# Moving four pieces of a two-block kernel: k's first tiles into the second transpositions, wider turns of k, the first attention gate ahead of q's last turn, scores inside the fourth attention gate

## What is computed

```python
h = concatenate([meta, x])                          # 16 + 1024 = 1040 positions
u = rmsnorm(h, norm_g)
f_in, f_gate, q, k, v, a_gate = split(u @ w_in)     # 512, 512, 512, 128, 128, 512
f_out = fourier_branch(f_in, w_fmix, b_fmix) * silu(f_gate)
q = apply_rope(rmsnorm(q, q_g), cos, sin)           # 8 heads of 64
k = apply_rope(rmsnorm(k, k_g), cos, sin)           # 2 heads of 64
s = q @ k.T * 64 ** -0.5
a_out = (softmax(s) @ v) * silu(a_gate)
h = h + concatenate([f_out, a_out]) @ w_out
h = rmsnorm(h, final_g)
# second block: stick-breaking attention, gated convolution, FFN
```

## Time and profile before

| | |
|---|---|
| median of 3 runs | 2277.32 us (2276.4 to 2278.12) |
| the profiled execution | 2277.11 us, its span 2275.1 us |
| PE busy | 2138.6 us (94%) |
| DVE / ACT / POOL busy | 50% / 37% / 30% |
| chain that ended last | PE 84%, DVE 10%, ACT 3%, issue 2%, DMA 1% |

### The profile page before, as it was taken

The page is one execution under the profiler, slowest core; times in us unless marked ns, Lnnn a source line. Parts: engine busy times, 40 slices in busy tenths (PEclk is TensorE's granted clock), DMA queues, the critical chain, the costliest instruction groups (busy, mean ns, idle before and its releaser), DMA issues.

```text
span 2275.1 us, 27632 instructions
## 1 busy us (share of the span) xinstructions
PE 2138.6 (94%) x10609; PEld 1769.5 (78%) x10609; DVE 1136.8 (50%) x1547; ACT 831.4 (37%) x1477; POOL 673.5 (30%) x527
## 2 busy tenths in 40 slices
PE   6898998999998999898998999989999999999996
...
DMA packets 142919, 164.65 MB, mean 72 GB/s; under 512 B 7091, under 2 KB 108999, under 8 KB 142823
## 3 DMA queue, kind: packets, MB, share of 16 engines
...
...
## 4 chain that ended last, share of the span: by engine, by line
PE 84%; DVE 10%; ACT 3%; issue 2%; DMA 1%; ACTq 0%; DVEq 0%
PE psum L589 18%; PE psum L591 18%; PE psum L590 17%; PE psum L886 15%; PE psum L798 3%; PE psum L809 3%; PE psum L824 1%; PE psum L825 1%; PE psum L826 1%; PE psum L923 1%; PE psum L907 1%; DVE softplus_part L1994 1%; PE psum L599 1%; PE psum L940 1%; PE psum L908 1%
## 5 line engine op out<-in xcount | busy, mean ns | idle before, releaser
L534 POOL TENSOR_TENSOR w_ring<-w_staging,zero 128x8 fp32r<-128x8 f32 x172 | 47.3, 275 | 1548.6 <-PE psum L591 1055.3
L537 POOL TENSOR_TENSOR w_ring<-w_staging,w_ring 128x1024 fp32r<-128x1024 f32 (+1 forms) x172 | 440.3, 2560 | 14.4
L886 PE MATMUL psum<-h,w_ring 128*128 128x512 f32 x1728 | 440.8, 406 | 0.7 <-ACT v L1380 0.7
L886 PEld LDWEIGHTS psum<-h,w_ring 128*128 128x128 f32 x1728 | 322.3, 193 | 69.3 <-ACT v L1380 1.1
L589 PE MATMUL psum<-ffn_in,w_ring 128*128 128x512 f32 x672 | 265.4, 395 | 0.0
L591 PE MATMUL psum<-ffn_in,w_ring 128*128 128x512 f32 x672 | 264.2, 393 | 0.0
L590 PE MATMUL psum<-ffn_in,w_ring 128*128 128x512 f32 x672 | 263.8, 393 | 0.0
L2116 DVE SCALAR_TENSOR_TENSOR up_buf<-psum,vectors,up_buf 128x1023 f32<-128x1023 f32 x44 | 56.4, 1283 | 308.3 <-ACT up_buf L1598 308.3
L535 POOL TENSOR_SCALAR w_ring<-w_staging 128x1016 fp32r<-128x1016 f32 (+1 forms) x172 | 183.0, 1064 | 0.0
L591 PEld LDWEIGHTS psum<-ffn_in,w_ring 128*128 128x128 f32 x672 | 126.0, 188 | 30.5
L590 PEld LDWEIGHTS psum<-ffn_in,w_ring 128*128 128x128 f32 x672 | 126.3, 188 | 29.3
...
## 6 DMA issues: line engine op xcount, KB each, us to landing
...
```

The source lines that it names most:

```text
L537: pool.tensor_tensor(lo[:, 0:width], WS[:, s, 0:width], plain(hi[:, 0:width]), ALU.subtract).then_inc(S["w_split"], 1)
L886: ins = pe.matmul(mix_bank(h), (sl if x == 2 else sh)[:, P * k:P * k + P], ml if x == 1 else mh, start=m == 0, stop=m == UNIT // 2 - 1)
```

## The change

- POOL makes the three MEMSETs of v_hi_ones_lo instead of DVE, as soon as the last tile of u is transposed, and two more chunks are split ahead of its loop, so that they stand before them.
- DVE normalises tiles 0 and 1 of the second transpositions amid the last four pairs of the DFT's results (`again`), each behind two pairs.
- Tiles 0 and 1 of k are squared, summed, guessed and rotated amid tiles 4 to 8 of the second transpositions (`k_square`, `k_guess` on ACT, `rotate`, `k_rotate` on DVE: the same instructions as before, named). Tiles 2 to 8 stay in the later loop.
- PE turns k's tiles 0 and 1 straight behind the last `kv_unit`; the other seven turns stand one behind every 15 products of the Fourier gates.
- `a_gate(0)` stands ahead of the last tile of q on ACT (`q_hi(TT - 1)`, line 1244 before) and on DVE (`q_lo(TT - 1)`, line 1866 before).
- PE's fourth attention gate is made in two halves, with `scores(1)` and `turn_probs(0)` between them. ACT makes `probs_hi(0)` in step 2, then the sigmoid of gate 3; DVE makes its MEMSET in step 1 and the product of gate 3 in step 3; the gate's store and the first loads of the gates move from steps 2 and 4 to 4 and 5.

```diff
-            peeled = C_KV + 2
+            peeled = C_KV + 4
...
+            pool.wait_ge(S["nt_mm"], N_A1 + KTILES)
+            pool.memset(plain(VV[:, TT, :, :]), 0.0).then_inc(S["vv_set"], 1)
+            pool.memset(plain(VV[:, 0:TT, :, DH:2 * DH]), 1.0).then_inc(S["vv_set"], 1)
+            pool.wait_ge(S["vv_set"], 2)
+            pool.memset(plain(VV[0:META, TT, :, DH:2 * DH]), 1.0).then_inc(S["vv_set"], 1)
...
-            def fm_unit(c, mov, banks, between=None):
+            def fm_unit(c, mov, banks, between=None, halves=range(2)):
...
-                for h in range(2):
+                for h in halves:
...
+            turn_k(0)
+            turn_k(1)
+
+            def turn_beside(f, m):
+
+                i = 2 * KT * f + m
+                if i % 5 == 4 and i // 5 + 2 < KTILES:
+                    turn_k(i // 5 + 2)
 
             for f in range(4):
                 if f == 1:
                     settle(tm=T_Q)
                 elif f == 3:
                     settle(fm=U_FGATE + 1)
-                fm_unit(C_FGATE + f, a1_half, F_GATE_PAIRS[f],
-                        lambda m: turn_k(4 * f + m // 4) if m % 4 == 3 and 4 * f + m // 4 < KTILES else None)
+                fm_unit(C_FGATE + f, a1_half, F_GATE_PAIRS[f], lambda m: turn_beside(f, m))
...
             pe.wait_ge(S["pr_done"], TT)
             scores(0)
             settle(fm=U_AGATE + 2)
-            fm_unit(C_AGATE + 3, a1_half, A_GATE_PAIRS[3])
+            fm_unit(C_AGATE + 3, a1_half, A_GATE_PAIRS[3], halves=range(1))
+            scores(1)
             settle(fm=U_AGATE + 3)
-            for i in range(1, HEADS * TT + 3):
+            turn_probs(0)
+            fm_unit(C_AGATE + 3, a1_half, A_GATE_PAIRS[3], halves=range(1, 2))
+            for i in range(2, HEADS * TT + 3):
...
+            def k_square(u):
+                rows = tokens_of(u)[1]
+                act.wait_ge(S["tm_free"], T_KV + u + 1)
+                act.activation(KSQ[0:rows, u % 2, 0:P], KV[0:rows, u, 0:P], ACT.Square).then_inc(S["pr_sq"], 1)
+
+            def k_guess(u):
+                guess(tokens_of(u)[1], 8 * (u % 2), KV_HEADS, 1.0 / DH, True)
...
+                if t in (4, 6):
+                    k_square(t // 2 - 2)
+                elif t in (5, 7):
+                    k_guess(t // 2 - 2)
...
+                    if u >= 2:
+                        k_square(u)
                     act.activation(VV[0:rows, u, :, 0:DH], KV[0:rows, u, P:2 * P].rearrange("p (g d) -> p g d", g=KV_HEADS),
                                    ACT.Copy).then_inc(S["kv_vhi"], 1)
-                    guess(rows, col, KV_HEADS, 1.0 / DH, True)
+                    if u >= 2:
+                        k_guess(u)
...
             a_gate(0)
+            q_hi(TT - 1)
             a_gate(1)
...
-                if i == 1:
+                if i == 2:
+                    act.wait_ge(S["pt_zero"], 1)
+                    probs_hi(0)
                     a_gate(3)
                     load_tables()
-                    act.wait_ge(S["pt_zero"], 1)
-                if i == 2:
+                if i == 4:
                     store_a_gate(3)
-                if i == 4:
+                if i == 5:
                     act.wait_ge(S["gate_stored"], 112)
                     load_a_gate(0)
                     load_a_gate(1)
...
+            def again(t, rows):
+                n = N_A1 + t
+                v.wait_ge(S[f"nt_in{n % 2}"], 16 * (t // 2 + 1))
+                normalise(N_A1, t, XIN[N_A1][0:rows, n % 2, :], RX[0:rows, t:t + 1], rows)
...
-            v.memset(plain(VV[:, TT, :, :]), 0.0).then_inc(S["vv_set"], 1)
-            v.memset(plain(VV[:, 0:TT, :, DH:2 * DH]), 1.0).then_inc(S["vv_set"], 1)
-            v.wait_ge(S["vv_set"], 1)
-            v.memset(plain(VV[0:META, TT, :, DH:2 * DH]), 1.0).then_inc(S["vv_set"], 1)
...
+                    if h and j % 2:
+                        again(j // 2, P)
...
+            for t in range(KTILES + 1):
+                if 2 <= t < KTILES:
+                    rows = tokens_of(t)[1]
+                    again(t, rows)
+                if t:
+                    lo_of_tile(N_A1 + t - 1, A1, *tokens_of(t - 1))
+                if t in (5, 7):
+                    rotate(t // 2 - 2, KSQ, P, KV_HEADS)
+                elif t in (6, 8):
+                    k_rotate(t // 2 - 3)
...
+                    if u >= 2:
+                        rotate(u, KSQ, rows, KV_HEADS)
...
-            for f in range(3):
-                a_gate(f)
+            a_gate(0)
+            q_lo(TT - 1)
+            a_gate(1)
+            a_gate(2)
...
-                if i == 0:
-                    a_gate(3)
+                if i == 1:
                     v.wait_ge(S["w_used"], C_OUT)
                     v.memset(plain(PT[:, :, KTILES - 1, :]), 0.0).then_inc(S["pt_zero"], 1)
                     v.wait_ge(S["pt_zero"], 1)
+                if i == 3:
+                    a_gate(3)
```

42 lines of the change are left out of this document (18 added, 24 removed).

## The result

The changed kernel takes 2263.47 us (median of 4 runs, 2260.71 to 2267.19) beside 2276.86 us for the kernel before (median of 4, 2275.61 to 2278.12): a ratio of 0.9943, 95% interval 0.993 to 0.9955, 13.4 us faster. The profiled execution took 2267.19 us with a span of 2265.2. It is the longest of the four, and a comparison of the two spans (9.9 us) would mislead, so I compare stages.

A forecast was written before the change was run, and what follows sets the result against it. PE, busy 94% of the span, was taken to bound the kernel. Fourier gates and k's turns 6.9, first attention gate 7.1 and attention entry 2.5 sum to 16.5 us won: 2260.8 us forecast, range 2257.5 to 2267.

The forecast's parts named there:

- the entry: Entry to the attention, fourth gate's end to scores 4: scores 4 start 13.4 us behind that end; 2.5 us won.
- Tile 2: Fourier gates: k's tile 2 ready 8.1 us behind the last product of k and v; PE waits 4.1 us.
- The low stretch behind it: Fourier gates, behind PE's wait for k's tile 2: a stretch at the low clock costing 1.8 us.
- the term of 6.9: Fourier gates and turns of k: q starts at 235.7 instead of 242.58, 6.9 us won.
- The end of the transpositions: End of the second transpositions: 0 taken, bounds a gain of 0.4 and a loss of 1 us; MEMSETs cost nothing.
- The first attention gate: PE's third attention gate: the whole wait for the first gate's product and its low stretch go, 7.1 us won.
- The third: Rival, attention entry: MEMSET held or low clock several steps longer; 2.5 turns into -2, time 2265; chance 0.12.
- the first: Rival, k's turns: splits catch tiles 5 and 8, MEMSETs delay; 2 us won, time 2265.8; chance 0.2.
- The fifth: Rival, attention: it stays at the low clock, slower; with 12 such steps the time is 2287; chance 0.03.
- The second: Rival, Fourier gates: the wait for k's tile 2 goes too, 4.1 + 1.8 us more, time 2255; chance 0.06.
- the fourth: Rival, first attention gate: ACT or DVE comes late to it, 7.1 us are gone, time 2268; chance 0.04.

The follow-up runs named there:

- e9: Changed kernel with the two splits that POOL makes from the last product of k and v on waiting for the rotation of k's tile 2; 2264.23 us.
- e7: Changed kernel with the fourth attention gate's sigmoid taken in two halves on ACT and its product on DVE ahead of step 3's maximum; 2262.11 us.
- e3: Kernel before with only the first attention gate moved ahead of q's last tile on ACT and DVE; 2270.46 us.
- e1: Changed kernel with its entry to the attention as before: fourth gate whole, scores 1 and the first transposition behind it; 2263.35 us.
- e10: Changed kernel with only DVE's product of the fourth attention gate moved ahead of the maximum of step 3; 2260.01 us.
- e2: Kernel before with the part on k alone: early tiles 0 and 1, wider turns, POOL's MEMSETs; 2268.76 us.
- e4: Changed kernel unaltered, measured again beside follow-up kernels; 2263.81 us.
- e6: Changed kernel with POOL's three MEMSETs also waiting for the rotation of k's tile 1; 2263.52 us.
- e11: Changed kernel with k's turns 2 to 8 again one behind every 12 products instead of 15; 2262.59 us.

## Why the prediction was right, and where it was off

2260.8 us was forecast and 2263.47 measured, inside the range. Part of that is luck: of the 16.5 us forecast the stages show 12.2 and the medians 13.4, the term of the entry is not there at all, and the range was wide enough to hold that. Two of the three terms were right in mechanism and near in size. The terms, in the order of the sum:

- **Tile 2: right.** Its turn starts at 192.51, 8.1 us behind K at 184.4, with a wait of 4.11 ended by k_rotated, and no other turn waits. e9 shows the reason, too: without the splits beside it, it is ready 5.1 us behind K (189.73, K at 184.6).
- **The low stretch behind it: mis-sized.** I took the 9 products of the kernel before, 1.8 us. It is 13 (192.8 to 198.3), 2.6 us. The 52.7 us that I had from K to q's first product are 53.8; e7, whose low stretch was shorter, has 52.73 from K to Q. So the term of 6.9 is 5.8.
- **The end of the transpositions: inside the bounds (-1), not 0.** The start brings 0.42, as foreseen (4.13 from f_out to the first transposition, 4.55 before). The transposition of tile 7 comes 0.28 late, as foreseen, too, the next one 0.4 late on top, and the MEMSETs on POOL cost 0.4: I excluded a hold because "a MEMSET reads nothing", which holds for two-input instructions but not for the TENSOR_SCALAR. They also last 1.6 us, not the 3.7 that I took from the rate of a split; a hold as long as I feared could not have come from them.
- **The first attention gate: right.** 7.1 forecast, 7.2 to 7.3 measured, alone (e3) and in the whole; DVE's product ends at 307.4, PE comes to the third gate 5.1 us later.
- **The entry: wrong, 2.5 forecast, nothing measured (e1).** Its first steps held: 2.04 us ahead of the gate's end (forecast 2.4), DVE's MEMSET of 0.91 beside a split, scores 3 at 7.8 behind the gate's end (7.5). The step that failed is the last one, scores 3 to scores 4, of which I wrote "it is 5.9 us now, at the low clock" and "I keep that", and that the product of gate 3 "is in the 5.9". It was 7.95, 2.05 more, of two parts. DVE makes the product behind the maximum of step 3 and the first attend waits for it: 0.9 us (e10). And the 5.9 were not all at the low clock, as I had read them: in the kernel before the clock rises within the fourth product of the first attend, which takes 2.2 us (363.79 to 366.02); wholly at the low clock, in the changed kernel, it takes 3.4 (350.41 to 353.78), 1.1 more. What is left of the 2.5 goes into step 4, which begins at the low clock. That the two orders come out even in the mean (e1) is measured; that the low clock is what evens them out is read from single executions and not tested alone.
- **The rivals.** The third's outcome, an entry that gives back its share, came to pass, but by neither of its two mechanisms: the MEMSET was not held, and the low clock lasted into step 4, not several steps more. Of the first, the longer low stretch and the MEMSETs' hold were real; no later tile waited at a split, and the hold was 0.4 us, not 1. The fifth (a step at the low clock again and again) did not come: from step 5 on the clock is full. The second, PE's wait for tile 2 gone, did not come either, nor the fourth.

What stays open is why a wait of the same length is followed by 9 or 13 products at the low clock. The traces show half of it. The stretches of the changed kernel (wait until 192.51) and of e7 (wait until 192.43):

```profile
191.60:192.50 0.90, 0.00 (x0) 0.00 (x0) 0.83 (x5) 0.00 (x0) 0.00 (x0) 0.50 0.76 134
...
191.40:192.35 0.95, 0.00 (x0) 0.00 (x0) 0.88 (x5) 0.00 (x0) 0.00 (x0) 1.00 0.75 86
192.40:195.80 3.40, 3.38 (x9) 2.73 (x10) 2.86 (x13) 1.56 (x6) 0.00 (x0) 0.50 0.33 127
```

In the changed kernel the clock has fallen while PE still waits, and then 13 products are slow; in e7 it falls only as the wait ends, and 9 are. The other profiles with a wait of 4 us or more there agree: where the clock fell 0.8 us or more ahead of the wait's end (e1, e2, e3, e4, e6, e10) it stayed low for 4.7 to 6.0 us behind it, where it fell later (the kernel before, e9, e11) for 3.2 to 4.2. What sets the moment of the fall no run shows. How much of the spread between executions it explains is open as well; the profiles of one program lie up to 5.2 us apart behind m6 alone, more than the terms that I argued about at the entry.
